# Query groups chained into one another in stick-breaking attention, and a reciprocal taken as Exp of minus Ln

## The reference

```python
# stick-breaking attention, 8 heads of 64, SEQ 8192; z = q.k / sqrt(64)
log_beta = jax.nn.log_sigmoid(z)
log_1mb = jnp.where(valid, jax.nn.log_sigmoid(-z), 0.0)
later = lax.cumsum(log_1mb, axis=3, reverse=True) - log_1mb
w = jnp.where(valid, jnp.exp(log_beta + later + log_rem[..., None]), 0.0)
acc = acc + jnp.einsum('bhqk,bhkd->bhqd', w, vblk)
log_rem = log_rem + jnp.sum(log_1mb, axis=-1)   # key blocks from the diagonal back
...
# sliding window of 128 keys, 8 heads, with a sink logit per head
p = jnp.exp(logits - m)
probs = p / (jnp.sum(p, axis=-1, keepdims=True) + jnp.exp(sink - m))
out = jnp.einsum('bnhgqk,bnkhd->bnqhgd', probs, vv)
```

## Time and profile before

| | |
|---|---|
| six runs, lowest, median, highest | 8408.93, 8577.89, 8596.48 us |
| the six runs | 8409.4, 8596.48, 8589.09, 8408.93, 8595.0, 8566.68 us |
| the profiled execution | 8408.58 us |
| its span on the slowest core (core 4), and on the others | 8406.9 us, 8370.4 to 8403.9 us |
| mean granted TensorE clock, lowest and highest core | 0.912, 0.917 |
| core 4, busy over the span: PE, ACT, DVE, POOL | 64%, 67%, 28%, 8% |
| core 4, 830 to 1290 us (`phase_B1`): PE, DVE, ACT busy | 134.9, 230.6, 75.9 us |
| core 4, 1290 to 6365 us (`phase_B2`): PE, DVE, ACT busy | 3182.1, 1125.4, 4715.3 us |
| share of the chain that ended last: `Gb`, `Xp`, `Yp`, `rec` | 19%, 19%, 9%, 1% |

### The profile page before, as it was taken

How to read it: one execution, slowest core, us unless ns; L and a number is a source line. 1 busy time by engine, 2 the same in 40 slices (tenths; PEclk the granted TensorE clock), 3 DMA queues, 4 the chain that set the end, 5 groups by cost and what they waited for, 6 DMA issues and landing times.

```text
span 8406.9 us, 85993 instructions; the slowest of 8 cores (8370.4 to 8406.9 us)
## 1 busy us (share of the span) xinstructions
PE 5420.6 (64%) x25468; PEld 2017.4 (24%) x25468; DVE 2381.0 (28%) x3522; ACT 5628.2 (67%) x6358; POOL 641.9 (8%) x622
## 2 busy tenths in 40 slices
PE   4896325666666666666666666666664676699678
PEld 1343222111112111112111112111111232244333
DVE  3221552222222222222222222222222222577612
ACT  2221116999998999998999998999994121465401
POOL 2221000000000000000000000000001121243200
PEclk9998667999998999998999998999997888799788
DMA  4333001000001000001000000000003212312243
GB/s 137 115 100 122 10 10 74 1 2 1 1 1 38 1 2 1 1 1 38 1 2 1 1 1 2 1 2 1 1 1 111 65 61 88 121 48 62 81 152 121
DMA packets 123651, 332.84 MB, mean 40 GB/s; under 512 B 10528, under 2 KB 41536, under 8 KB 118464
## 3 DMA queue, kind: packets, MB, share of 16 engines
q1 hardware_dynamic: 94640, 220.51, 8.1%
q0 software_dynamic: 28560, 106.85, 4.0%
HBM read 220.49 MB, written 106.83 MB: 39 GB/s over the span
## 4 chain that ended last, share of the span: by engine, by line
PE 59%; ACT 24%; issue 6%; DMA 5%; DVE 5%; POOL 1%; SPq 0%; ACTq 0%; DVEq 0%; POOLq 0%
ACT Gb L202 19%; PE Xp L507 19%; PE Yp L507 9%; PE psA L180 7%; PE Zp L180 7%; PE psU L180 6%; PE psC L180 5%; PE psD L180 4%; ACT Eb L202 1%; DMA xsC<-xT 1%; DVE rec L451 1%; ACT PB L202 1%; DVE LG L224 1%; DVE ybU L224 1%; PE OPs L180 1%
## 5 line engine op out<-in xcount | busy, mean ns | idle before, releaser
L208 DVE TENSOR_TENSOR Wb<-Eb,Gb 128x1024 bf16<-128x1024 bf16 (+2 forms) x1728 | 1103.0, 638 | 3920.6 <-ACT Gb L202 3882.2
L507 PE MATMUL Xp<-Lb,triC 128*128 128x512 bf16 (+3 forms) x3384 | 955.8, 363 | 1819.4 <-ACT Gb L202 1818.8
L202 ACT ACTIVATE Eb<-Zp,kbias_s 128x1024 bf16<-128x1024 f32 (+2 forms) x1728 | 1764.2, 1021 | 164.4 <-PE Zp L180 159.0
L202 ACT ACTIVATE Lb<-Eb 128x1024 bf16<-128x1024 bf16 (+2 forms) x1728 | 1675.3, 969 | 163.2 <-ACT Eb L202 6.3
L202 ACT ACTIVATE Gb<-Xp 128x1024 bf16<-128x1024 f32 (+2 forms) x1728 | 1590.6, 920 | 44.6 <-PE Xp L507 42.4
L507 PE MATMUL Yp<-Wb,Vt 128*128 128x512 bf16 (+4 forms) x3456 | 979.5, 366 | 44.9 <-DVE Wb L208 44.6
L507 PE MATMUL Xp<-Lb,tri 128*128 128x512 bf16 (+4 forms) x3456 | 982.0, 365 | 0.5
L507 PEld LDWEIGHTS Xp<-Lb,triC 128*128 128x128 bf16 x3384 | 219.4, 96 | 2528.5 <-issue 2528.4
L180 PE MATMUL Zp<-QTt,KTt 64*128 64x512 bf16 (+4 forms) x3456 | 696.1, 374 | 29.4 <-DMA QTt<-QTs 27.3
L180 PE MATMUL psU<-hTU,WU 128*128 128x512 bf16 (+1 forms) x3168 | 628.6, 358 | 28.0 <-DVE ybU L224 26.3
L224 DVE SCALAR_TENSOR_TENSOR ybU<-psU,cw_s,ybU 128x510 f32<-128x510 f32 (+1 forms) x792 | 528.0, 690 | 75.5 <-ACT ybU L202 16.2
(11 more groups left out here) (107 smaller groups left out, 3656.1 us busy)
## 6 DMA issues: line engine op xcount, KB each, us to landing
xsA<-xT SPq DMA_DIRECT2D x16, 2048.0 KB, 11.1
stgU<-w_up SPq DMA_DIRECT2D x32, 704.0 KB, 7.0
aTD<-ATs SPq DMA_DIRECT2D x8, 2816.0 KB, 17.8
ATs<-aTU POOLq DMA_DIRECT2D x8, 2805.0 KB, 14.7
VSs<-stV POOLq DMA_DIRECT2D x64, 256.0 KB, 3.4
Vt<-VSs SPq DMA_DIRECT2D x8, 2048.0 KB, 9.1
xsC<-xT SPq DMA_DIRECT2D x8, 2048.0 KB, 15.6
X1s<-x1C POOLq DMA_DIRECT2D x8, 2048.0 KB, 16.3
```

Of the source, the lines that this page charges most:

```text
L202: return e.activation(out.ap, in_.ap, func, **kw)
L208: S.op(eng, lambda e: e.tensor_tensor(out.ap, a.ap, b.ap, op), reads=[a.buf, b.buf], writes=[out.buf])
L507: return lambda e: e.matmul(out.ap, lhsT.ap, rhs.ap, start=start, stop=True, skip_group_check=True)
```

## The change

In `phase_B1` the reciprocal on DVE is replaced by two ACT functions, Ln of `den` into a new buffer `lden`, and Exp of minus that into `rec`.

In `phase_B2` a group becomes an object with two parts. `pre` holds the first scores and the first Exp and Ln, `run` holds the clearing and the rest. The groups of all four head pairs stand in one list, and each one's `run` calls the `pre` of the next ahead of its own last `s_G`. Buffers are numbered through over the whole list (`ubase`) rather than from 0 in each group; since every `U` is a multiple of four, each step gets the buffer that it had before. Loads of a head pair's buffers are issued behind the last group that reads the old contents.

```diff
@@ phase_B1
+        lden = P.sb("lden", [128, 512], F32)
...
-            S.op("dve", lambda e: e.reciprocal(rec.t[:], den.t[:]), reads=[den.buf], writes=[rec.buf])
+            act(None, lden[:], den[:], AF.Ln)
+            act(None, rec[:], lden[:], AF.Exp, scale=-1.0)
@@ phase_B2
+            def pre():
                 s_Z(0)
                 if U > 1:
                     s_Z(1)
                 s_EL(0)
                 if U > 2:
                     s_Z(2)
+
+            def run(nxt):
+                S.op("pe", [mmx(X[:, r, 0:n], ident[:], zb[:, 0:n], True) for r in range(2)],
+                     reads=[ident.buf, zb.buf], writes=[X.buf])
+                S.op("pe", [mmx(Yp[:, 0:n], ident[:], zb[:, 0:n], True)],
+                     reads=[ident.buf, zb.buf], writes=[Yp.buf])
                 s_A(0)
                 for t in range(U):
                     if t + 1 < U:
                         s_EL(t + 1)
+                    if t == U - 1 and nxt is not None:
+                        nxt.pre()
                     s_G(t)
                     if t + 1 < U:
                         s_B(t)
...
+        load_hp(0)
+        load_hp(1)
+        glist[0].pre()
+        for i, g in enumerate(glist):
+            nxt = glist[i + 1] if i + 1 < len(glist) else None
...
+            g.run(nxt)
+            if nxt is not None and nxt.hp != g.hp and nxt.hp + 1 < 4:
+                load_hp(nxt.hp + 1)
```

More of the change, by code:

```diff
@@ L484, in load_hp @@
             load(QTt[s][:], QTs[hp, :, :])
[L486 to L562, removed]
@@ new lines, in phase_B2, with make_group, c0of, mmx @@
+        class Grp:
+            pass
+        def make_group(hp, qs, n, ycol, gidx, ubase):
+            G = Grp()
+            sl = hp % 2
+            Kt, Vv, Qt = KTt[sl], Vt[sl], QTt[sl]
+            qc = qs - (NH - 1) * 512
+            kbmax = (qs + n - 2) // 128
+            kbs = list(range(kbmax, -1, -1))
+            U = len(kbs)
+            G.U = U
+            Yp = Y[gidx % 2]
+            ye = yev[gidx % 2]
+            def c0of(u):
+                j = kbs[u] - qs // 128
+                return 128 * j if (n == 512 and j >= 1) else 0
+            def mmx(out, lhsT, rhs, start):
+                return lambda e: e.matmul(out.ap, lhsT.ap, rhs.ap, start=start, stop=True,
+                                          skip_group_check=True)
+            def s_Z(u):
+                kb = kbs[u]
+                j = kb - qs // 128
+                c0 = c0of(u)
+                Zt = Z[(ubase + u) % 2]
+                for r in range(2):
+                    po = 64 * r
+                    prs = [(Kt[po:po + 64, kb * 128:(kb + 1) * 128], Qt[po:po + 64, qc + c0:qc + n])]
+                    if j >= 0:
+                        if n == 512:
+                            prs.append((ident[:], dmask[:, j, c0:n]))
+                        else:
+                            prs.append((ident[:], dmask[:, 0, 126:128]))
+                    pe_group(Zt[:, r, c0:n], prs)
+            def s_EL(u):
+                kb = kbs[u]
+                b = (ubase + u) % NBUF
+                c0 = c0of(u)
+                act(None, Eb[b][:, :, c0:n], Z[(ubase + u) % 2][:, :, c0:n], AF.Exp, scale=0.125,
+                    bias=kbias[:, kb:kb + 1])
+                act(None, Lb[b][:, :, c0:n], Eb[b][:, :, c0:n], AF.Ln, bias=1.0)
+            def s_A(u):
+                b = (ubase + u) % NBUF
+                c0 = c0of(u)
+                fns = [mmx(X[:, r, c0:n], tri[:], Lb[b][:, r, c0:n], False) for r in range(2)]
+                S.op("pe", fns, reads=[tri.buf, Lb[b].buf], writes=[X.buf])
+            def s_B(u):
+                b = (ubase + u) % NBUF
+                c0 = c0of(u)
+                fns = [mmx(X[:, r, c0:n], triC[:], Lb[b][:, r, c0:n], False) for r in range(2)]
+                S.op("pe", fns, reads=[triC.buf, Lb[b].buf], writes=[X.buf])
+            def s_G(u):
+                b = (ubase + u) % NBUF
+                c0 = c0of(u)
+                act(None, Gb[b][:, :, c0:n], X[:, :, c0:n], AF.Exp, scale=-1.0)
+                tt("dve", Wb[b][:, :, c0:n], Eb[b][:, :, c0:n], Gb[b][:, :, c0:n], ALU.mult)
+            def s_Y(u):
+                kb = kbs[u]
+                b = (ubase + u) % NBUF
+                c0 = c0of(u)
+                fns = []
+                for r in range(2):
+                    fns.append(mmx(Yp[:, c0:n], Vv[:, kb, 128 * r:128 * (r + 1)], Wb[b][:, r, c0:n], False))
+                S.op("pe", fns, reads=[Vv.buf, Wb[b].buf], writes=[Yp.buf])
+            def pre():
@@ L584, in phase_B2 @@
                 store(YSB[:, hp, ycol:ycol + n], ye[:, 0:n])
+            G.pre = pre
+            G.run = run
+            return G
+        glist = []
+        ub = 0
+        for hp in range(4):
+            for (qs, n, ycol) in groups:
+                g = make_group(hp, qs, n, ycol, len(glist), ub)
+                ub += g.U
+                g.hp = hp
+                glist.append(g)
+        load_hp(0)
[4 more added lines that the diff above has]
+            if nxt is not None and nxt.hp != g.hp and nxt.hp + 1 < 4:
+                pass
+            g.run(nxt)
+            if nxt is not None and nxt.hp != g.hp and nxt.hp + 1 < 4:
+                load_hp(nxt.hp + 1)
         S.barrier()
```

## The result

The changed kernel took 8336.05 us, median of ten runs (8308.87 to 8435.8); the kernel before now has twenty runs with a median of 8575.88 (8404.22 to 8682.97). The ratio of the comparable runs is **0.9914, interval 0.9889 to 0.994**: 50 to 93 us less than 8409. The profiled execution took 8306.08 us, 102 less than the profiled one of before.

A forecast was written before the change was run, and what follows sets the result against it. phase_B1 was taken as bound by a serial chain per block, phase_B2 by ACT, with stops at group boundaries. From 8408.6 us, minus 64 (reciprocal) and 22 (boundary order), gave 8323 us; range 8255 to 8505.

The forecast's parts named there:

- The reciprocal: phase_B1: Ln and Exp on ACT take 2.38 us where 4.32 stood; 1.94 us a block, 64 us over 33 blocks.
- The order at a boundary: phase_B2, between groups: reordered queues save 0.68 us a boundary, 22 us over 32 (18 to 24); waits 2.3 and about 1.2.
- rival (4): phase_B2 boundaries: PE's stops make it pass at 1.2 GHz, slower than before, 8433 us; chance 0.05.
- rival 1: phase_B2: the overlap fills both ACT stops at group boundaries, 64 + 140 us less, 8204 us; chance 0.04.
- rival 2: phase_B1: Ln and Exp make ACT reload its function table twice a block, 85 us, no change at 8408; chance 0.05.
- Clock: phase_B1: PE's burst keeps its clock as shown, worth nothing; at the other end twice the clock, 64 us less.
- rival (3): phase_B1: the shorter block lets PE's burst run at 2.4 GHz, up to 64 us more saved, 8259 us; chance 0.14.
- the upper bunch: Whole-kernel runs before: four of six from 8567 to 8596 us, two at 8409; a changed median there reads 158 to 187 more.
- the 20 us that would have spoken against the whole: Outside phase_B1 and phase_B2: the prediction is wrong as a whole if something there moves by more than 20 us.

The follow-up runs named there:

- the two moves in the queue: Changed kernel with the next group's first scores, and its Xp clearing and first sum, queued ahead of old-group work: ratio 0.9791, lowest 8238.05 us.
- the blocks overlapped: The two moves in the queue, plus phase_B1's next-block scores, LG and PB issued ahead of this block's products: ratio 0.9622, lowest 8083.99 us.
- the product late: The blocks overlapped, plus yst (the product with the reciprocal) issued one block later, with two rec: ratio 0.9503, lowest 8004.70 us.

## Why the prediction was right, and where it was not

**The reciprocal** (forecast 64 us). Right: 63.7 us on core 0 over the 32 distances, 61.8 to 62.8 on the other seven cores, and alone as well as with the overlap. `den` to `yst` took 2.31 us where 2.38 was worked out from `phase_A`'s rows, and nothing took the reciprocal's place. That the price is paid on the path was shown by doing it twice.

**The order at a boundary** (forecast 22 us, waits of 2.3 and a little over 1). The mechanism was right to a tenth of a microsecond: waits of 2.39 and 1.23, 6.81 us from `Gb` to `Gb` where 6.90 was forecast. The term was sized too small: `phase_B2` is 28.6 us shorter on core 0 and 27.5 to 36.5 over the eight cores, where 18 to 24 was given. Measured as the prediction does, from the end of the last but one `Gb` to the new group's first, the boundaries themselves give 24.5 us on core 0: the 28 between tile groups go from 7.61 to 6.84 us in the mean, the four from a pair to a tile from 7.00 to 6.09, and the three to a pair, which were set to nothing, from 5.59 to 5.81. What the sum left out lies behind the boundaries: the idle time ahead of the full-width `Eb` falls from 10.6 to 4.5 us on core 0, and from 8.2 to 15.7 on the eight cores to 4.4 or 4.5 on all. (Together 30.6; ACT's own instructions took some 2 us longer.) These are the waits of the earlier trace rows, which were counted only as what rival (4) would add, not as what the forecast would take away. With Ln and Exp alone they stand as before, 11.2 us, and with the overlap alone they are down to 4.2, so they belong to the order.

**The overlap fills both stops** (rival 1). It does not, and the two moves in the queue show that most of it could have come, 111 of the 140 us: the first stop was the scores' place behind the old sums, the second the clearing's place behind the last value products. The prediction's sentence against this rival, that the new `Xp` cannot be cleared before the last `Gb` has read the old one, is true, but the wait that it was made to explain was mostly the value products, which did not have to stand there.

**Table loads** (rival 2). None came, in 33 blocks or with four functions a block. The Trainium skill ("ScalarE: Activation LUTs", Table sets: the hidden batching unit) names a set that holds both exp and ln; the rows agree, 33 loads before and after.

**Clock.** In B1 it stayed as the forecast took it. Of the 1024 products into `OP` and `DN` between the first and the last `den`, 1014 to 1024 began at the low clock before and 1005 to 1011 after, over the eight cores; the matmuls at 2.4 GHz were nearly all scores, which have time to spare. So rival (3) did not come. The Trainium skill's rule ("TensorE: Matmul & The Clock Gate", Part 1) that activity raises the clock was what spoke for (3); with the shorter block the mean clock of this stretch is 0.600 to 0.609 over the cores, against 0.586 to 0.625, and the section on the hardware has a run that goes the other way.

At a boundary itself the clock is 1.00 as before, so rival (4) did not come either. But behind the boundaries it did change, and the other way round. Before, it fell to the low level 2.7 to 10.3 us after the first `Eb` of the new group on core 0, at 27 of the 28 boundaries between tile groups, where PE had just stood still for 1.61 and 1.34 us. The wait of the earlier trace rows on core 4 stands in such a stretch:

```profile
1866.00:1868.00 2.00, 2.00 (x6) 0.50 0.02 4
```

In the changed kernel PE stands still for 1.61 and 0.77 us, and the clock falls 9.4 to 12.7 us after the first `Eb`, at 20 of the 28. Of the waits of over 0.3 us ahead of a full-width `Eb`, twelve on core 0 before, only the four behind the boundaries from a pair to a tile are left. Why the clock falls later was not tried.

**The base of the number.** This is the step that failed. The sum starts from one execution, 8408.6 us, and puts no term on where the changed kernel's runs would lie; the text adds only that a median in the upper bunch would read 158 to 187 us more. The median of the kernel before stayed in its upper bunch (8575.88 over twenty runs); the changed kernel's ten runs lie from 8309 to 8387 with one at 8436, and none where that sentence put the upper bunch, near 8490. So 8323 is 13 us from the median that came, and that is luck: set against the median of before it reads as 3% less, of which the working argues 1.0% and the comparable runs show 0.86%. Nothing shows that the edits took the upper bunch away: with one of them alone most runs lay high again (8474.63 to 8595.59 in five of six, 8541.6 to 8610.45 in seven of eight).

What was forecast was a difference of 86 us to a named execution: 99 to 102 came in the profiles, 50 to 93 in the timed runs. The two agree where the clock is alike. The changed kernel's three runs with a granted clock of 0.918 or more on every core took 8308.87 to 8315.19 us, 89 to 106 less than the seven lowest of before (8404.22 to 8415.21). The other six that are compared, up to 8386.72, each have cores at 0.906 to 0.916; why those got less is open. So on a like clock the sum was 13 to 16 us too small: on core 0, 7 of that lie in the term for the boundaries and 6 in the later phases, which scatter.

**Outside the two phases.** From the end of `phase_B2` to the end of the span core 0 takes 6.1 us less and core 4 12.2, but core 3 takes 11.1 and core 6 13.7 more. It scatters by that much between cores and kernels whose code there is the same, so this part is not counted to the change; no core moved by the 20 us that would have spoken against the whole.

## What to carry to other kernels

Where queues are strict orders, an overlap is worth what its place in each queue allows: write down, for the engine that waits, what stands ahead of the awaited instruction in the other engine's queue. Here that gave two waits to within a tenth of a microsecond. A change that "overlaps" may only move a wait: here two stops of 1.26 and 3.11 us became two of 2.39 and 1.23, and moving the scores and the clearing past the old group's products took another 82 us on top of 29. A block that is a chain over three engines gained more from being run beside the next one (11.72 to 6.79 us, and to 4.80 with a higher clock) than from a faster link (13.71 to 11.72). And a difference is forecast against a base: where the runs of a kernel fall in two bunches, say which of them the forecast is held against, since the bunches lie further apart here (some 160 us) than the change is large.

## What the hardware showed that was not expected

With the blocks overlapped, PE works for two thirds of the stretch and yet has the lower clock throughout; with the product late, at about the same busy time, it has 0.86 (length, then busy us and count of PE, PEld, DVE, ACT and POOL, then the granted clock). The first row is of the run with overlapped blocks:

```profile
870.00:1010.00 140.00, 94.44 (x987) 84.69 (x987) 72.60 (x63) 69.42 (x81) 14.91 (x21) 0.50 0.09 21
```

and this of the run with the product late:

```profile
850.00:990.00 140.00, 90.21 (x1392) 81.37 (x1388) 102.41 (x89) 100.48 (x117) 20.59 (x29) 0.86 0.12 29
```

A matmul takes longer at the lower clock (four took 0.63 us and 0.39 above), so the counts compare better than the busy times: 987 and 1392 matmuls. Before, a stretch of the same phase had 0.62 with 54 matmuls in 14 us, some 540 in 140, and PE busy for a third of it. So more work of PE in a stretch did not by itself bring the higher clock. Why one run gets it and the other not was not tried.
